# The experts' weights: two transfers of 1 MB into each slot become one of 2 MB

## The reference, cut to what matters

```python
def moe_swiglu(u, w_router, wg, wu, wd):
    bsz, seq, d = u.shape
    xf = u.reshape(bsz * seq, d)
    logits = (xf @ w_router).astype(F32)
    vals, idx = lax.top_k(logits, TOP_K_EXPERTS)
    w = jax.nn.softmax(vals, axis=-1)
    gate = jnp.sum(jax.nn.one_hot(idx, N_EXPERTS, dtype=F32) * w[..., None], axis=1)
    y = jnp.zeros_like(xf)
    for e in range(N_EXPERTS):
        y = y + gate[:, e:e + 1].astype(xf.dtype) * swiglu_2(xf, wg[e], wu[e], wd[e])
    return y.reshape(bsz, seq, d)

def swiglu_2(u, wg, wu, wd):
    return (jax.nn.silu(u @ wg) * (u @ wu)) @ wd
```

## Time and profile before

| what | value |
|---|---|
| time, median of 3 runs | 2890.52 us |
| lowest and highest | 2889.07 and 2897.74 us |
| span of the profiled execution | 2892.9 us |
| TensorE matmul busy | 2712.1 us (94%) |
| VectorE busy | 2001.7 us (69%) |
| ScalarE busy | 1488.3 us (51%) |
| mean granted TensorE clock | 0.953 |
| moved by the DMA engines | 674.26 MB |

### The profile page before, as it was taken

The page is one execution under the profiler, slowest core; times in us unless marked ns, Lnnn a source line. Parts: engine busy times, 40 slices in busy tenths (PEclk is TensorE's granted clock), DMA queues, the critical chain, the costliest instruction groups (busy, mean ns, idle before and its releaser), DMA issues.

```text
span 2892.9 us, 33028 instructions
## 1 busy us (share of the span) xinstructions
PE 2712.1 (94%) x13394; PEld 2133.6 (74%) x13394; DVE 2001.7 (69%) x2297; ACT 1488.3 (51%) x1663; POOL 121.4 (4%) x172
## 2 busy tenths in 40 slices
PE   6998899999989878998899999999999999999997
PEld 3766577777766557777777777778888888888886
DVE  4565465446547545557754566688989999999998
ACT  4332364345344234335543444666666666767665
POOL 3013000000000300000000000000000000000000
PEclk8998899999989879999999988899999999999999
DMA  7443545666555355652356533189999999999996
GB/s 265 175 150 103 185 172 200 226 224 220 188 175 189 119 202 184 229 191 99 108 200 231 190 105 117 66 300 361 352 361 357 351 352 359 363 348 361 357 360 229
DMA packets 292877, 674.26 MB, mean 233 GB/s; under 512 B 19462, under 2 KB 115846, under 8 KB 259440
## 3 DMA queue, kind: packets, MB, share of 16 engines
q1 hardware_dynamic: 286944, 664.35, 64.7%
q0 software_dynamic: 4912, 6.67, 0.8%
q10 hardware_dynamic: 864, 1.06, 0.1%
HBM read 670.93 MB, written 1.10 MB: 232 GB/s over the span
## 4 chain that ended last, share of the span: by engine, by line
PE 81%; DVE 10%; ACT 6%; DMA 2%; issue 1%; SPq 0%; POOL 0%; ACTq 0%; DVEq 0%; POOLq 0%
PE psum L544 22%; PE psum L546 21%; PE psum L545 21%; PE psum L76 9%; PE psum L378 3%; DVE wslot_r L554 2%; PE psum L1452 1%; PE psum L2979 1%; DVE cacc L76 1%; PE psum L1587 1%; PE psum L2002 1%; DMA first<-in_w_mod 1%; DVE dec L76 1%; DVE x L76 1%; ACT whi_r L76 1%
## 5 line engine op out<-in xcount | busy, mean ns | idle before, releaser
L544 PE MATMUL psum<-whi_r,xhi_r 128*128 128x512 f32 (+1 forms) x752 | 301.5, 401 | 12.8 <-DVE dslot_r L554 8.3
L546 PE MATMUL psum<-whi_r,xlo_r 128*128 128x512 f32 (+1 forms) x752 | 293.2, 390 | 0.0
L554 DVE TENSOR_TENSOR wslot_r<-wslot,whi_r 128x2048 fp32r<-128x2048 f32 (+1 forms) x114 | 255.5, 2251 | 53.5 <-ACT whi_r L76 51.3
L545 PE MATMUL psum<-wslot_r,xhi_r 128*128 128x512 f32 (+1 forms) x736 | 287.2, 390 | 0.0
L554 DVE TENSOR_TENSOR wslot_r<-wslot,arena_r 128x2048 fp32r<-128x2048 f32 x113 | 258.4, 2287 | 31.0 <-ACT arena_r L2923 30.4
L554 DVE TENSOR_TENSOR dslot_r<-dslot,wide_r 128x2048 fp32r<-128x2048 f32 x110 | 251.4, 2285 | 28.1 <-ACT wide_r L2937 27.9
L2923 ACT ACTIVATE arena_r<-wslot 128x2048 fp32r<-128x2048 f32 x112 | 215.0, 1919 | 94.1 <-DMA wslot<-in_moe_w_gate 47.1
L2937 ACT ACTIVATE wide_r<-dslot 128x2048 fp32r<-128x2048 f32 x110 | 210.7, 1918 | 97.6 <-DMA dslot<-in_moe_w_down 97.4
L554 DVE TENSOR_TENSOR dslot_r<-dslot,ld_hi_r 128x2048 fp32r<-128x2048 f32 x44 | 100.6, 2292 | 187.5 <-ACT ld_hi_r L76 187.5
L76 ACT ACTIVATE whi_r<-wslot 128x2048 fp32r<-128x2048 f32 (+1 forms) x114 | 212.1, 1874 | 26.4 <-DVE wslot L76 9.4
L545 PE MATMUL psum<-wslot_r,arena_r 128*128 128x512 f32 x560 | 220.8, 394 | 0.0
(11 more groups left out here) (547 smaller groups left out, 6112.2 us busy)
## 6 DMA issues: line engine op xcount, KB each, us to landing
wslot<-in_moe_w_gate SPq DMA_DIRECT2D x112, 1024.0 KB, 5.1
wslot<-in_moe_w_up SPq DMA_DIRECT2D x112, 1024.0 KB, 5.0
dslot<-in_moe_w_down SPq DMA_DIRECT2D x110, 1024.0 KB, 4.9
dslot<-in_w_mod SPq DMA_DIRECT2D x35, 1024.0 KB, 4.9
wslot<-in_w_gate SPq DMA_DIRECT2D x66, 512.0 KB, 5.5
wslot<-in_w_up SPq DMA_DIRECT2D x66, 512.0 KB, 6.2
dslot<-in_w_down SPq DMA_DIRECT2D x33, 1024.0 KB, 5.0
mod_half<-in_w_ada SPq DMA_DIRECT2D x27, 1024.0 KB, 4.8
```

Source lines behind the costliest of these rows:

```text
L544: t.matmul(out_, hi, w_hi, start=start, stop=False)
L545: t.matmul(out_, hi, w_lo, start=False, stop=False)
L546: return t.matmul(out_, lo, w_hi, start=False, stop=stop)
L554: return v.tensor_tensor(one_pass(lo), src, one_pass(hi), ALU.subtract)
```

## The change

In the experts' stage each slot gets one transfer of 2 MB in place of two of 1 MB. It is issued when TensorE is done with both halves of the slot. There are three transfers a piece instead of six, and one semaphore for each slot. ScalarE's rounding, VectorE's remainders, the tiles' places and sizes and the matmuls stay as they were, by halves. `both_d` is the two down slots seen as one tile.

```diff
-    def load_w(g, c, half):
+    def load_w(g, c):
         if g >= 1:
-            nc.sync.wait_ge(q_up, 4 * (g - 1) + 2 * c + half + 1)
+            nc.sync.wait_ge(q_up, 4 * (g - 1) + 2 * c + 2)
         e, i_ = divmod(g, per)
-        nc.sync.dma_start(raw(c, half).rearrange("p (k n) -> p k n", k=4),
-                          gv[c][:, e, 4 * half:4 * half + 4, i_ * WIDE:(i_ + 1) * WIDE]).then_inc(w_sem[c][half], 16)
-
-    def load_d(g, part):
+        nc.sync.dma_start(ws[c].ap[:].rearrange("p (k n) -> p k n", k=KD),
+                          gv[c][:, e, :, i_ * WIDE:(i_ + 1) * WIDE]).then_inc(w_sem[c][0], 16)
+
+    both_d = at("both_d", 38624, 4096)
+
+    def load_d(g):
         if g == GW - 1:
-            nc.sync.wait_ge(q_up, 4 * g + part + 1)
-            dst, sem = raw(0, part), w_sem[0][part]
+            nc.sync.wait_ge(q_up, 4 * g + 2)
+            dst, sem = ws[0].ap[:], w_sem[0][0]
         else:
             if g >= 1:
-                nc.sync.wait_ge(q_dn, 2 * (g - 1) + part + 1)
-            dst, sem = ds[part].ap[:], ds[part].sem
-        nc.sync.dma_start(dst.rearrange("p (k n) -> p k n", k=2), dv[:, 2 * g + part]).then_inc(sem, 16)
+                nc.sync.wait_ge(q_dn, 2 * g)
+            dst, sem = both_d[:], ds[0].sem
+        nc.sync.dma_start(dst.rearrange("p (i k n) -> p i k n", i=2, k=2), dv[:, 2 * g:2 * g + 2]).then_inc(sem, 16)
...
     def load_w_after():
         sp.wait(ws[1].reader)
-        for half in range(2):
-            load_w(0, 1, half)
-        for part in range(2):
-            sp.wait(ds[part].reader)
-            load_d(0, part)
+        load_w(0, 1)
+        sp.wait(ds[0].reader, ds[1].reader)
+        load_d(0)
...
         def high_w(g, c, half):
-            a.wait_ge(w_sem[c][half], w_n0[c][half] + 16 * (g + 1))
+            a.wait_ge(w_sem[c][0], w_n0[c][0] + 16 * (g + 1))
             if g >= 1:
                 a.wait_ge(q_up, 4 * (g - 1) + 2 * c + half + 1)
...
         def high_d(g, part):
             if g == GW - 1:
-                a.wait_ge(w_sem[0][part], w_n0[0][part] + 16 * (GW + 1))
+                a.wait_ge(w_sem[0][0], w_n0[0][0] + 16 * (GW + 1))
                 a.wait_ge(q_up, 4 * g + part + 1)
             else:
-                a.wait_ge(ds[part].sem, d_n0[part] + 16 * (g + 1))
+                a.wait_ge(ds[0].sem, d_n0[0] + 16 * (g + 1))
...
         def sync_step(s):
             for c in range(2):
-                for half in range(2):
-                    if s + 1 < GW:
-                        load_w(s + 1, c, half)
-            for part in range(2):
-                if 1 <= s < GW:
-                    load_d(s, part)
+                if s + 1 < GW:
+                    load_w(s + 1, c)
+            if 1 <= s < GW:
+                load_d(s)
```

More of the change, by code:

```diff
@@ L2738, in experts_slots @@
         sp.wait(ws[0].reader)
-        for half in range(2):
-            load_w(0, 0, half)
+        load_w(0, 0)
     off[0] = 0
@@ L2912, in d_raw @@
         def d_raw(g, part):
-            return raw(0, part) if g == GW - 1 else ds[part].ap[:]
+            return raw(0, part) if g == GW - 1 else both_d[:, part * 2048:(part + 1) * 2048]
         def high_of_d(g, part):
@@ L3282, in moe_first @@
             ws[u].n += 16 * (GW + 1 - u)
-            wl_[u].n += 16 * (GW + 1 - u)
-            ds[u].n += 16 * (GW - 1)
             ws[u].reader, ds[u].reader = (q_up, 4 * GW), (q_dn, 2 * GW)
+        ds[0].n += 16 * (GW - 1)
     def moe(c):
```

## The result

The changed kernel takes 2984.1 us (median of 4 runs, 2978.5 to 2984.3) against 2889.8 us before (2886.1 to 2897.7): a ratio of 1.034, interval 1.031 to 1.036, 94 us slower. The forecast was 79 us slower. The profiled execution has a span of 2982.7 us, 89.8 over the one of before.

What follows compares the result with a forecast made beforehand. TensorE was taken to bound the kernel. 54 down loops of 18.7 us against 17.63 (+58), late landings (+16) and the start (+4) made +78, 2969 us for the median; range 2935 to 3015.

Steps and rivals of the forecast that it cites:

- 3.7 us to spare for down: Experts' stage before the change: VectorE ends `split_h` at 2385.51, TensorE begins `downs` at 2389.19, so down has 3.7 us slack.
- Which loop: Experts' stage: down's slot loop of 18.7 us becomes the step; gate's loop of 17.5 us hides under it.
- The loop's length: Down's slot, from `downs` through issue, transfer, rounding, remainder and `split_h` to the next `downs`: 18.7 us, bounds 18.4 and 19.2.
- the transfer of 2 MB: Down's transfer in its loop: 4.85 us for the first MB plus 2.45 for the second, 7.3 us.
- 5.8 + 5.65: Down's loop without its transfer: 5.8 us from first `downs` matmul to issue, 5.65 from landing to the next `downs`.
- Late landings: Down's transfers in the experts' stage: 3 in 10 of 54 land 1.0 us late, +16 us, bounds 0 and 27.
- the clock's rival: TensorE's stalls before `downs` halve its clock in half of 28 ordinary steps: +39 us, about 3008; chance 0.17.
- 4 forecast: Start of the experts' stage: gate of piece 1 is issued whole and lands later, ending at 1909.5 instead of 1905.59, +4 us.
- add nothing: End of the stage: last piece's down weights go into the gate slot, issued about 12 us before they are wanted, 0 us.
- Hidden anyway: 2 MB land so soon that down's loop fits TensorE's step, second MB costing 0.9 us: 2890 us; chance 0.07.
- The shorter transfer: Down's transfer takes 7.0 us with hardly a late landing: +46 us, about 2936; chance 0.15 for 2900 to 2950.

Runs made afterwards that it cites:

- The runs with one delay alone: Kernel before with only late issue (both 1 MB halves issued once the slot is free), or only joint landing (rounding waits for both halves): 2904.2 and 2904.5 us.
- the run with both: Kernel before, still 1 MB transfers, both issued when the whole slot is free and rounding begun only when both have landed: 2969.4 us, ratio 1.029.

## Why the prediction was right, and where its numbers were off

**What bounds the kernel before: right.** TensorE, with 3.7 us to spare for down. The runs with one delay alone show that this slack is real, and the run with both fits its size: 5.3 us of delay less 3.7 is 1.6 over an ordinary step of 17.07, and the typical step there was 18.9.

**Which loop: right.** Down's, not gate's, though gate is wanted first in a step. Down alone in one transfer costs all of it; TensorE waits for `split_h` in each step and hardly for gate or up. That `split_h` stands in the loop was shown by moving it out (down's round falls to 17.9 to 18.2) and by putting a remainder ahead of it (21.25).

**The loop's length: 18.7 forecast, 19.15 typical.** The step of the sum that was mis-sized is the transfer of 2 MB: 7.3 taken from pairs of 1 MB, 7.7 measured, inside the stated bounds of 7.0 to 7.8. It is 54 x 0.35 = 19 us. The rest, 5.8 + 5.65, measured 11.5 against 11.44. The other rule weighed there, the fit of 2.0 us plus bytes over 436 GB/s from the Trainium skill ("DMA: Bandwidth & Descriptors", Anatomy of one DMA), gives an estimate of 6.8 us for 2 MB; the measured 7.7 decides.

**Late landings: 16 us forecast, about none for down.** Its landings span 7.3 to 8.1 us; none is 1 us over the median in this trace. The transfer put too short and the late landings put too dear nearly cancel in the sum, which is luck: both together were put at 19.0 us a step, and the average round was 19.33.

**What makes up the last 0.2 us.** A few rounds are longer by about 1.7 us. In the windows after, TensorE is idle for more than half of the first and gets half the clock in the second (columns as in the earlier trace rows):

```profile
1959.60:1963.00 3.40, 1.51 (x8) 1.05 (x7) 3.37 (x4) 1.97 (x3) 0.00 (x0) 1.00 0.90 294
1963.00:1966.40 3.40, 3.40 (x9) 2.66 (x8) 3.40 (x3) 2.45 (x2) 0.00 (x0) 0.50 1.05 408
```

So the clock's rival took part in five of 54 steps, 17 us of the stage at 1.2 GHz up to the transposes of piece 54, about 8 us lost. That case had stood at 39 us and a chance of 0.17.

**Sum over the profiled executions.** Ahead of gate 1's transfer -13.2 us (1878.93 against 1892.15; the code there is the same, and the kernel before wandered by 12.4). From there to the transposes of piece 0 +6, with 4 forecast. The 54 steps +90, with 74 forecast for loops and late landings. After the transposes of piece 54 +7, with 0 forecast. The prediction priced nothing there (the last piece's down weights "add nothing"), but piece 54's own late down costs 1.8 us before the next transposes and pushes VectorE's last split back: the stall ahead of the last `downs` grew from 1.51 to 5.31 us. -13 + 6 + 90 + 7 = 90. The stage itself became 103 us longer, and the profiled pair shows less because of what lies ahead of it. Held against the 103, the forecast of 78 was 25 us short; that it missed the measured 94 by only 15 is luck in part.

**The rivals.** Hidden anyway: fell, the second MB costs 2.5 to 2.8 us and not 0.9. That the DMA engines look full (0.99 in the earlier trace rows) meant nothing: with the change they move less, 325 GB/s. The shorter transfer: fell, with landings of 7.7 us where it had 7.0.

**Left open.** Why the runs with one delay alone are 22 us slower when their stage has 11 and 14; one profile of each can't tell the rest from the wander. Why one transfer of 2 MB lands 0.35 us after the second of two of 1 MB. No version faster than the kernel before was tried: TensorE has no idle time in its steps that an edit of the transfers could give back.

## What to carry to other kernels

Where each slot is the only buffer of its block, it goes round a loop of freeing, transfer, preparation and use, and joining two halves lengthens that loop twice: the issue waits for the later half's reader and the first use for the later half's bytes. Compare the sum of both with the slack between the prepared half and its use, and include whatever the preparing engine does in between (here a split that has nothing to do with the weights). A busy share near 1 on the DMA engines doesn't say that they are the bound: look at whether SP waits before it issues.

## What was not expected of the hardware

One transfer of 2 MB (7.7 us median for down) lands later than two of 1 MB issued 0.4 us apart (7.3 us for both). The time ahead of the stage, with the same instructions, differed by 12.4 us between two executions of one kernel. Regular stalls of up to 2.3 us ahead of `downs` were followed by matmuls at 1.2 GHz in 5 of 54 steps, those five stalls being 1.8 to 2.3 us long, while others of up to 1.9 us were not; with stalls of 2.7 to 5.5 us it was 43 of 54.
